# In the expert loop ScalarE issues the loads of the down matrices, and the sync engine those of gate and up

## The reference, cut to what matters

```python
scores = sigmoid(h @ w_router); top 8 of 64 per token; gates = normalised scores * 2.5
for e in range(64):
    hg, hu = h @ w_gate_e[e], h @ w_up_e[e]                   # 1024 x 256 each
    out += (silu(hg) * hu * gates[:, e:e+1]) @ w_down_e[e]    # 256 x 1024
out += swiglu(h, w_gate_s, w_up_s, w_down_s) + x1             # the shared expert and the residual
```

## Time and profile before

| | |
|---|---|
| median of 3 runs | 1101.09 us (1101.03 to 1101.51) |
| profiled execution | 1100.27 us; span in the trace 1098.5 us |
| PE busy | 1082.1 us, 99% of the span |
| DVE, ACT, POOL busy | 882.6, 739.8, 289.6 us |
| granted TensorE clock, mean | 0.997 of full speed |
| DMA | 284.71 MB, 259 GB/s over the span |

### The profile page before, as it was taken

How to read it: one execution, slowest core, us unless ns; L and a number is a source line. 1 busy time by engine, 2 the same in 40 slices (tenths; PEclk the granted TensorE clock), 3 DMA queues, 4 the chain that set the end, 5 groups by cost and what they waited for, 6 DMA issues and landing times.

```text
span 1098.5 us, 19485 instructions
## 1 busy us (share of the span) xinstructions
PE 1082.1 (99%) x5823; PEld 893.6 (81%) x5823; DVE 882.6 (80%) x1405; ACT 739.8 (67%) x1304; POOL 289.6 (26%) x288
## 2 busy tenths in 40 slices
PE   8999999999999999999999999999999999999996
PEld 7789988877777887678888888888888888888885
DVE  6534386478865845589999999999999999999994
ACT  5434464544346522168888888888888888888884
POOL 1221021000000001125433333333333443444332
PEclk9999999999999999999999999999999999999998
DMA  8243212421532093679999999999999999999982
GB/s 251 78 116 104 90 45 72 154 77 40 135 115 97 0 389 125 254 262 370 389 388 382 383 377 378 382 387 390 382 385 384 369 391 376 383 376 378 377 297 39
DMA packets 97354, 284.71 MB, mean 259 GB/s; under 512 B 19684, under 2 KB 22252, under 8 KB 96925
## 3 DMA queue, kind: packets, MB, share of 16 engines
q1 hardware_dynamic: 78876, 250.52, 60.0%
q0 software_dynamic: 18432, 33.61, 12.4%
HBM read 279.79 MB, written 37.81 MB: 289 GB/s over the span
## 4 chain that ended last, share of the span: by engine, by line
PE 91%; DVE 5%; ACT 1%; DMA 1%; issue 1%; POOL 1%; POOLq 0%; SPq 0%; ACTq 0%
PE bank L1850 32%; PE bank L1671 23%; PE bank L1864 17%; PE bank L1878 5%; PE bank L1824 3%; PE bank L1613 3%; PE bank L1838 3%; PE bank L1858 1%; DVE w_lo L1093 1%; PE bank L1698 1%; PE bank L1727 1%; PE bank L1740 1%; PE bank L1937 1%; PE bank L1716 1%; DMA arena<-in_x 1%
## 5 line engine op out<-in xcount | busy, mean ns | idle before, releaser
L1850 PE MATMUL bank<-gu_parts,xT_parts 128*128 128x512 f32 x1280 | 338.7, 394 | 0.0
L1850 PEld LDWEIGHTS bank<-gu_parts,xT_parts 128*128 128x128 f32 x1280 | 235.4, 188 | 45.9
L1864 PE MATMUL bank<-w_lo 128*128 128x512 f32 x804 | 201.6, 399 | 0.0
L1864 PEld LDWEIGHTS bank<-w_lo 128*128 128x128 f32 x804 | 146.3, 188 | 28.5 <-issue 0.5
L606 POOL TENSOR_TENSOR turn<-minus_half 16x1 f32<-16x1 f32 x123 | 69.9, 568 | 340.8 <-ACT arena L932 167.6
L617 POOL DMA_INDIRECT out<-arena,idxs x64 | 122.5, 1915 | 49.7 <-DMA out<-arena,idxs 20.4
L1671 PE MATMUL bank<-w_hi,hT_hi 128*128 128x512 f32 (+1 forms) x320 | 124.7, 390 | 1.4 <-DVE arena L1188 0.7
L1671 PE MATMUL bank<-w_hi,hT_lo 128*128 128x512 f32 (+1 forms) x320 | 121.8, 380 | 0.0
L1671 PE MATMUL bank<-w_lo,hT_hi 128*128 128x512 f32 (+1 forms) x320 | 121.5, 380 | 0.0
L1453 DVE TENSOR_TENSOR gu_parts<-arena,gu_parts 128x1024 fp32r<-128x1024 f32 x96 | 117.1, 1220 | 0.3 <-PE bank L1838 0.3
L1453 DVE TENSOR_TENSOR gu_parts<-arena_x,gu_parts 128x1024 fp32r<-128x1024 f32 x96 | 117.1, 1220 | 0.1
(11 more groups left out here) (228 smaller groups left out, 1908.4 us busy)
## 6 DMA issues: line engine op xcount, KB each, us to landing
arena<-in_w_gate_e SPq DMA_DIRECT2D x64, 512.0 KB, 8.9
arena<-in_w_up_e SPq DMA_DIRECT2D x64, 512.0 KB, 10.8
arena<-in_w_down_e SPq DMA_DIRECT2D x64, 512.0 KB, 7.3
arena_x<-in_w_gate_e SPq DMA_DIRECT2D x64, 512.0 KB, 9.0
arena_x<-in_w_up_e SPq DMA_DIRECT2D x64, 512.0 KB, 11.3
arena_x<-in_w_down_e SPq DMA_DIRECT2D x64, 512.0 KB, 7.6
arena<-in_w_in SPq DMA_DIRECT2D x14, 1024.0 KB, 5.4
arena<-in_w_gate SPq DMA_DIRECT2D x8, 1024.0 KB, 5.7
```

The source lines that it names most:

```text
L1850: last = nc.tensor.matmul(out_, a[:, PER * c + j, :], b[c][:, :, j, :], start=(c == 0 and j == 0 and i == 0), stop=(c == CHUNKS - 1 and j ...
L1864: last = nc.tensor.matmul(psY[h][0:rows, :], midT[n][a][:, j, 0:rows], w[b][:, j, h * 512:(h + 1) * 512], start=(j == 0 and k == 0), stop= ...
```

## The change

`load_w` moves out of SP's block and takes a queue. SP's loop loses its wait for `wd_ready` and the two DMAs behind it. ACT's `step` gets, right behind the silu of expert k, a wait for `wd_ready` at 2(k + 1), that is, for expert k - 1's down matrix to be split, and the two DMAs of expert k + 3's down matrix. Loads of experts 7 to 63 move (57 of 64 pairs); the first seven stay on SP.

```diff
+        def load_w(n, k, e, queue=None):
 ...
+            for i in range(2):
+                (queue or nc.sync).dma_start(dst[...], src[...]).then_inc(w_in_sem[n][k], 16)
 ...
-                sp.wait_ge(wd_ready, 2 * (n + 2))
-                load_w(n, 2, 4 + n)
+                if n < 3:
+                    sp.wait_ge(wd_ready, 2 * (n + 2))
+                    load_w(n, 2, 4 + n)
 ...
                     load_w(n, 0, k)
                     load_w(n, 1, k)
-                    sp.wait_ge(wd_ready, read_d)
-                    load_w(n, 2, k)
 ...
-            def step(it, n, slot, more=True):
+            def step(it, n, slot, more=True, load=True):
 ...
                 silu_i(it, n)
+                if more and load:
+                    act.wait_ge(wd_ready, 2 * (k + 1))
+                    load_w((slot + 3) % 4, 2, k + 3, nc.scalar)
```

More of the change, by code:

```diff
@@ L389, in yT_of @@
             return yTa[k] if k < 2 else yTb[:, k - 2, :]
+        def load_w(n, k, e, queue=None):
+            t = (w_gate_e, w_up_e, w_down_e)[k]
+            src = t[bass.ds(e, 1)].rearrange("o (p j) f -> p (o j) f", p=P)
+            dst = (wgu[n][:, 0], wgu[n][:, 1], wd[n])[k]
+            rows = (HALF, HALF, NF // 2)[k]
+            for i in range(2):
+                (queue or nc.sync).dma_start(dst[:, i * rows:(i + 1) * rows], src[:, i * rows:(i + 1) * rows]).then_inc(w_in_sem[n][k], 16)
         block = ctx.enter_context(nc.Block())
@@ L493, in _ @@
             sp.dma_start(gffn_row, g_ffn.rearrange("(o d) -> o d", o=1).broadcast_to([P, D])).then_inc(gffn_in, 16)
[L495 to L502, removed]
             sp.wait_ge(merged_ready, ND)
@@ L545, in _ @@
                 load_w(n, 1, 4 + n)
-                sp.wait_ge(wd_ready, 2 * (n + 2))
-                load_w(n, 2, 4 + n)
-            regs = [sp.alloc_register(f"turn_value{i}") for i in range(2)]
+                if n < 3:
+                    sp.wait_ge(wd_ready, 2 * (n + 2))
+                    load_w(n, 2, 4 + n)
+            reg = sp.alloc_register("turn_value")
             with sp.Fori(2, E // 4) as m:
@@ L552, in _ @@
                     k = 4 * m + n
[L553 to L556, removed]
+                    sp.reg_mov(reg, CHUNKS * (k - 3))
+                    sp.wait_ge(gu_lo_ready, bass.RuntimeValue.of_register_unchecked(reg, min_val=1, max_val=2 * 16 * E))
                     load_w(n, 0, k)
                     load_w(n, 1, k)
-                    sp.wait_ge(wd_ready, read_d)
-                    load_w(n, 2, k)
             more = sp.value_load(rounds_i[0:1, 0:1], min_val=0, max_val=ROUNDS - 1)
@@ L1030, in _ @@
             for it in range(SH + 1, SH + 4):
-                step(it, it % 2, it % 4)
+                step(it, it % 2, it % 4, load=False)
             with act.Fori(SH // 4 + 1, ITEMS // 4 - 1) as m:
@@ L1035, in _ @@
             for it in range(ITEMS - 4, ITEMS):
-                step(it, it % 2, it % 4, more=it + 1 < ITEMS)
+                step(it, it % 2, it % 4, more=it + 1 < ITEMS, load=it + 3 < ITEMS)
             y_i(ITEMS - 1, 1)
```

## The result

The changed kernel takes 1115.21 us (median of 1111.76, 1115.21 and 1119.97), beside 1101.3 us (1101.03 to 1102.09) for the kernel before: ratio 1.0131 [1.0111, 1.0151]. All ratios leave out executions that took over 1.5% more than the fastest of the same kernel, here one of 2778.72 us that nothing recorded explains (with it the median is 1117.59). The kernel is slower, and in the way that the prediction had as its first rival. The profiled execution, the longest of the three, has a span of 1118.2 us, 19.7 us more than before.

The account below looks back on a forecast made before the run. PE, busy 19.05 of 19.05 us, was taken to bound the expert loop at 9.52 us a step. 1100.27 us plus 0 - 0 + 0, with the runs' median 0.82 us above, gave 1101.1 us; range 1099.0 to 1116.0.

Parts of the forecast that it names:

- first rival: Late in the loop, longer scatter landings become the bound: +0.3 us in 44 steps, 13 us, 1114 us; chance 0.27.
- no change: Whole kernel: PE stays busy throughout the expert loop, nothing gained or lost, 1101.1 us; chance 0.50.
- ACT's issue: Behind the silu, wait and issues take 0.95 us, delaying L976 by 0.14 to 0.52 us; 0 us on PE.
- The down load itself, and SP: Down pair starts about 1.8 us later, gate and up 5.2 us earlier on SP; both 0 us.
- ACT's stall: Late in the loop, ACT's down pair issue takes 2.01 us; about 12 steps cost 10 us, 1111 us; chance 0.10.
- my sign: Evidence for stalling on ACT: late DMA issues over 0.5 us each, and DVE idle before L1446.
- the term for the scatters: Scatters in the loop: added landing counted as 0 us, though bounds of 0 and 3.5 us were given.
- The rival's own working: Scatter chain: 1.5 us on top of a landing, so a 9.52 us step bears a landing of 8.0 us.
- Late gate and up: Gate and up loads arrive late, perhaps 1 us in each of the last 4 steps, 1105 us; chance 0.06.
- Less disturbance: PE's matmuls run faster beside spread loads: 57 x 0.055 = 3.1 us saved, 1098 us; chance 0.07.
- The test I set: Middle of the loop: the forecast is wrong if steps take 9.55 us or more.
- the case's own range: Whole kernel if nothing changes: 1100.0 to 1103.2 us, the top allowing 0.04 us in each of 57 steps.

Follow-up runs that it names:

- e4: Changed kernel with the experts' scatters replaced by a small POOL instruction, leaving their results out of the output: 1098.15 us, ratio 0.9973 to the kernel before.
- e5: Kernel before with the experts' scatters replaced by a small POOL instruction, leaving their results out of the output: 1098.03 us, ratio 0.9973.
- e2: Changed kernel, but SP again waits for the old down matrix's split before loading gate and up: 1105.97 us, ratio 1.0052 to the kernel before.
- e6: Changed kernel with one DMA of each down pair on ACT, the other on SP behind the silu: 1102.84 us, ratio 1.0015 to the kernel before.
- e9: Kernel before plus a wait and two unused 4 KB DMAs per step on ACT behind the silu: 1106.17 us, ratio 1.0047.
- e0: Changed kernel run once more, unedited: 1106.64, 1117.75, 1138.34 and 1146.71 us, too far apart for a ratio.
- e1: Changed kernel with the down pair issued by SP once the silu has run, ACT issuing nothing: 1099.80 us, ratio 0.9995 to the kernel before.
- e7: Changed kernel with ACT's wait and down pair issues moved behind the result copies: 1183.93 us, ratio 1.0664 to the kernel before.

## Why the prediction was right in its range and wrong in its sum

The range, 1099.0 to 1116.0 us, holds the 1115.21 us by 0.8 us. It reaches so far up only because of the first rival, which had a chance of 0.27. The likeliest value, no change at 1101.1 us (0.50), and the sum behind it miss by 14 us.

**ACT's issue: right.** Predicted 0.84 us for the pair plus a tenth, hidden behind ACT's wait for PE. Measured 0.83 us, starting inside the silu (the lower of my two bounds) or, late, before it, which I had not thought of, with L972 still waiting 0.84 us for PE; e4 equal to e5 says the same in time.

**The down load itself, and SP: right.** The pair lands in 7.6 to 7.8 us in the median (7.3 to 7.6 before) and nobody waits for it. The 5 us of lead for gate and up earned nothing.

**ACT's stall: fell.** Three of 114 DMA issues on ACT took more than the 0.5 us of my sign (0.57, 0.65 and 0.66), none more, and DVE waited 0.2 us in all for L1445 (L1446 in the kernel before). The stalls of the earlier trace rows stayed with SP.

**"No change": wrong, at the term for the scatters.** This is the step that failed. I put the added landing at 0 in the sum, although my own row gave bounds of 0 and 3.5 us, and gave the rival 0.27. The argument against it was that the pair is in flight at another time of the step than most of the scatter. It is not: the pair takes 7.7 us and a scatter 8.8, together more than a step of 9.52, so they overlap wherever they stand. The packets in the trace say how far: while one of the scatters 20 to 36 is in flight, 1.05 MB move on q10, the whole pair. That sum was to be had from the earlier trace rows before the run. The other half of the argument, "it held PE up nowhere before", only said that there was a store of lag, not that there was none to lose.

**The rival's own working: mechanism right, sizes off in ways that cancel.** I had 44 steps at +0.3 us, 13 us in all. What happened is 25 steps at +0.78 us (19.5 / 25). The landings of scatters 3 to 20 grew by 0.8 us, yet cost PE nothing. The overhead between landing and next start shrank from 1.42 to 0.97 us and took up half of it: it was no fixed cost but partly POOL waiting for its result. The other half lengthened the chain's steps by 0.37 us, 6 us of lag over 17 steps, and the two result buffers bore that. With an overhead of 0.86 us a step bears a landing of 9.52 - 0.86 = 8.66 us, not 8.0; the 1.5 us in my sum came from the one long turn of the earlier trace rows. Scatters 20 to 36 land in 8.69 us, right on that edge, and the late ones, at 9.48, are past it. ACT waits from 878 us on. That the rival's 1114 us lie within 2 us of the measured time is luck of these sizes: 0.3 us in 44 steps for 0.78 us in 25.

**Late gate and up: underrated.** At 0.06 it looked like a detail. It did not show in the profile after, but it makes up most of the waiting for DMAs in e2, e6, e9 and e0. The lead of 30.6 us was held against a median landing of 10.8 us, while the queue's worst is what counts: the slowest load, an up matrix, took 20.3 us from issue to landing before, and takes 26.2 us in the changed kernel. All loads of line 398, after:

```profile
DMA to landing us min/median/max: 3.8/9.1/26.2
```

**Less disturbance: fell.** Nothing of it in any run; no kernel with the whole of the work came out under before by more than e1's 0.05%.

**The test I set.** "Steps of 9.55 us or more in the middle of the loop" would not have caught this: the middle stayed at 9.53. A loss that first has to use up a buffer shows at the end of the loop, and that is where to look. (The upper end of the case's own range, 1103.2, should by its own working be 1101.1 + 57 x 0.04 = 1103.4 us.)

What is shown: the loss goes with the down pair back in SP's queue (e1) and without the scatters (e4, e5), runs through long landings and ACT's wait for a result buffer (trace, the four executions), and depends strongly on the phase (e7). What is not shown: what lengthens the late landings. That the DMA engines' alternation between queues does it is only argued, and one reading speaks against it in its plain form. While a late scatter (37 to 57) is in flight, 0.84 MB move on q10 in the changed kernel and it lands in 9.48 us; in e0 it is 0.99 MB and 8.80 us, in e2 1.04 MB and 8.59 us. More of the second queue beside the scatter goes with shorter landings there.

## What to carry to other kernels

When the DMA engines are full (share near 1) and a short, latency-bound transfer runs serially beside the bulk, moving bulk to another issuing engine may not be free even if its sequencer is idle: it changes the streams beside the short one, and their phase. Compute landing plus overhead of the serial chain against the step, with the overhead taken from a place where the chain lags, and treat a margin like the one here (8.66 - 8.15 = 0.5 us) as none. Count the buffers in between as a delay of the loss, not as its cover, and judge late steps, not middle ones.

## What was not expected of the hardware

- The same 59.78 MB in SP's queue or in one of their own: 1099.80 us (e1) or 1115.21. The Trainium skill, DMA: Bandwidth & Descriptors, section Issuing engines are not separate DMA queues, says that issuing on several engines only saves the sequencer's time. That holds for e4 and e5, without scatters; with them the measurement decides, and it says that moving the pair to the second queue can also cost 1.3%, in another phase 6.6%.
- Two DMAs of 4 KB a step in a queue of their own cost 0.47% (e9).
- A DMA issue on ACT starts while the ACTIVATE ahead of it still computes (944.09 us, with the silu running from 943.87 to 944.25), and late in the loop even 1.09 us before that ACTIVATE starts (954.26 for 955.35).
